# Queries and keys as block products, and attention's steps regrouped among the k tiles

## The chip, the cores and the metric

The kernel runs on one core of a Trainium2 chip. The metric is the time of one execution on the device, in microseconds (us). The median of three runs of the kernel before is 1344.37 us (1343.51 to 1346.86).

## What is computed

One layer of a decoder for two groups of tokens, 512 of a new prompt and 8 x 8 of samples with a paged past, 576 together, at a model width of 1024, all in float32:

```python
h = _rmsnorm(x, g_attn)
zq, zk, zv, zu, zs, zm, zg = jnp.split(h @ w_in, offs, axis=-1)
o_da = _da_prompt(q, k, v, ...)        # 8 heads; p1 - lam * p2, both softmax; RMSNorm of each head's output
o_sg, vn = _spatial_gate(jax.nn.gelu(zu), jax.nn.gelu(zs), sg_norm, sg_w, sg_b)
o_mx = _cross_attn(zm, mem_k, mem_v)   # 4 heads into 256 memory tokens
merged = gates[0] * (o_da @ w_branch[:1024]) + gates[1] * (o_sg @ ...) + gates[2] * (o_mx @ ...)
x = x + merged @ w_out
a, b = jnp.split(_rmsnorm(x, g_ffn) @ w_up, 2, axis=-1)
x = x + (jax.nn.silu(a) * b) @ w_down
```

`zq` and `zk`, `h` times two 1024 x 1024 blocks of `w_in`, are computed first and are used by the differential attention of prompt and samples; `zk` and `zv` are outputs too.

## The kernel before

**Panels.** Every product with a weight is cut into panels: 128 output features by 576 tokens, kept transposed (features on the partitions). `T` is 576, `HT` half of it, 288; `KT` is 8, the number of 128-row k tiles of the width. Float32 precision comes from a split: weights and activations are each a rounded high part and a low remainder, and each product is hi*hi + hi*lo + lo*hi. A k tile of a panel is therefore 3 x 2 matmuls of 128x288, and a panel of 8 k tiles is 48 matmuls (`panel`, L1895). Two accumulator pairs `acc[0]`, `acc[1]` alternate by panel. `split_hi` (L696, ACT) rounds the weights of the panel two ahead into `w_hi`, `split_lo` (L1183, DVE) subtracts that from `w_raw` into `w_lo`; SP (`stream`, `load_w`) loads `w_raw`, one DMA per panel of 0.5 MB, after the `w_lo` before it in that buffer is made. ACT evacuates a finished panel.

**Stages.** `STAGES` lists them: `mk`, `mv` (keys and values of the memory), `s` (spatial gate's v half, 8 panels), `q`, `k`, `v`, `u`, `da_gate` (8 panels each), `sg_branch` (16), `zm`, `da_proj`, `mx_gate`, `mx_proj`, `w_out` (8 each), then the feed-forward net: `up` and `down`. Behind the panels stand the smaller matmuls: `turn_tile` transposes a tile of `s` and `v` into token order (DVE's `nat_copy` takes it out), `mix` (L2053) does the spatial gate's 128x128 products behind the `k` panels, each waiting for its predecessor's `mix_bias` on DVE.

**Pairs.** The `up` stage has another form. A unit computes a pair of panels of 22 (`FT`) with a seven-product scheme for 2x2 blocks: the four blocks are two halves of the width by two 288-token halves, combined into sums and differences on both sides. A unit is `NJ` = 7 products of 4 (`KH`) k tiles and three matmuls each, 84 instead of 96 (`product`, L2349). For it DVE forms the weight sums (`pair_sums`) and low parts (`lo_of`), ACT the high parts (`hi_of`, L1061) and copies of products 0, 1 and 2 (`product_copy`, L1070), and DVE adds the products from PSUM into the two outputs. The activations' sums are made once (`xs_raw`, `xs_hi`, `xs_lo`). The weight sums of the first unit are formed on POOL (L1873) after the last `w_out` panel but one. All engines' loops over units are written out by hand and meet by counters: `pair_hi_done`, `pair_lo_done`, `pair_mm`, `pair_copied`, `pair_out`. At the end of the last unit ACT and DVE split the weights of down panels 0 and 1; then `g_hi` (ACT, L1137) and `g_lo` (DVE, L1684) tiles are made, and the first down panel (`down_panel`, L2376) waits for each k tile of them.

**Attention behind the gate panels.** Prompt attention is 32 tiles (`TILES_P`), four query blocks for each of eight heads, in the order `TILE_ORDER` of widths; tile n is in head n // 4. For a tile: `p_score` (L2088, TensorE, two products into two banks), `p_logits` (DVE, L1369, a minimum of each row), `p_exps` (ACT, L843), `p_combine` (DVE, L1394 to L1402, gives `a_p`), `p_turn_probs` (TensorE, L2098, transposes `a_p`, one to four blocks), `p_turned` (ACT, L866, copy to `aT_p`), `p_values` (TensorE, L2107). For a head: `p_copy` (ACT, L872), `p_squares` (ACT, L880), `p_norm` (DVE, L1409), `p_turn_out` (TensorE, L2079) and `p_output` (ACT, L886). There is one score buffer: `p_score(n)` waits for `p_logits(n-1)`. There is one turn buffer: `p_turn_probs(n)` waits for the `aT_p` copy of n-1. TensorE puts a step in front of each k tile of the gate panels: `p_step(q)` with q = 8c + k - 2 for k tile k of panel c. ACT and DVE have the same steps in program order, with each panel's evacuation (L702), `split_hi` and `split_lo` among them, so a step that comes late on one of them holds what stands behind it. The samples' attention follows behind `sg_branch`, the memory attention behind `da_proj` (samples) and `mx_gate` (prompt: `prompt_step(h, slot)`, 16 slots for a head in two panels, with `c_score` L2272, `c_turn_p` L2282, `c_values` L2288). `m_turn_o` (L2247) turns a sample's `o_m`, which DVE makes (L1501).

## Time and profile before

| | |
|---|---|
| median of three runs | 1344.37 us |
| the profiled execution | 1343.05 us |
| its span | 1341.3 us |
| TensorE busy | 98% of the span |
| VectorE (DVE) busy | 50% |
| ScalarE (ACT) busy | 39% |
| GpSimd (POOL) busy | 7% |
| DMA, mean over the span | 134 GB/s |
| granted TensorE clock, mean | 0.992 |

The span is the time between the first and the last record; what lies around it (1.75 us) is start and end. In a timeline each row is one instruction, or several of one kind that follow each other, with the time of its start, its length, engine, line, operation and tiles; in square brackets stands the idle time of the engine before it and the engine that ended it. Lengths of matmuls in sequence overlap, so distances are read from start to start. PE is TensorE.

### The profile page before, as it was taken

How to read it: one execution, taken by the hardware profiler on the slowest of the kernel's cores; microseconds unless marked ns; L12 is line 12 of the kernel's file. 1: busy time of each engine (PE TensorE's matmuls, PEld its weight loads, DVE VectorE, ACT ScalarE, POOL GpSimd, SP SyncE). 2: the span in 40 equal slices, each digit the busy share in tenths (PEclk: the TensorE clock that was granted, in tenths of full speed). 3: DMA queues.
4: the chain of work that ended last, by engine and by line, in shares of the span. 5: the costliest groups of instructions: out<-in, count | busy, mean ns of one | idle time of the engine just before them, and what ended most of it. 6: DMA issues, size and time to landing. Idle time of an engine off the chain costs nothing.

```text
span 1341.3 us, 25811 instructions
## 1 busy us (share of the span) xinstructions
PE 1315.5 (98%) x10082; PEld 1245.4 (93%) x10082; DVE 667.9 (50%) x1167; ACT 524.5 (39%) x1010; POOL 89.9 (7%) x129
## 2 busy tenths in 40 slices
PE   8899999999999999999999999998999999999997
PEld 8889999999888888888988889998999999999997
DVE  6643232223566532222344323567888888863333
ACT  5432321223477632222422343245555555552220
POOL 3620000000001010000000000001000000000001
PEclk9999999999999999999999999998999999999998
DMA  6544222524222197776589111432222222222221
GB/s 240 165 154 163 81 87 76 197 102 150 71 75 71 53 304 226 260 247 207 195 321 342 61 48 48 148 106 72 93 94 94 94 94 94 94 79 90 84 94 71
DMA packets 82087, 179.10 MB, mean 134 GB/s; under 512 B 5869, under 2 KB 40941, under 8 KB 80982
## 3 DMA queue, kind: packets, MB, share of 16 engines
q1 hardware_dynamic: 77750, 158.31, 34.7%
q10 hardware_dynamic: 2496, 12.58, 2.6%
q0 software_dynamic: 1760, 7.08, 1.5%
q8 instruction: 57, 0.93, 0.3%
q14 instruction: 24, 0.20, 0.0%
HBM read 166.13 MB, written 14.18 MB: 134 GB/s over the span
## 4 chain that ended last, share of the span: by engine, by line
PE 62%; issue 31%; DVE 2%; POOL 2%; ACT 1%; DMA 1%; POOLq 0%; SPq 0%; DVEq 0%; ACTq 0%
PE acc L1895 49%; PE ps L2107 2%; PE ps L2088 2%; PE ps L2164 1%; PE ps L2141 1%; PE ps L2272 1%; POOL ssum L1765 1%; PE ps L2288 1%; PE ps L2098 1%; PE ps L2239 1%; PE ps L1922 1%; PE ps L2053 1%; PE ps L2221 1%; DVE w_lo L1183 0%; DMA m_x<-memT 0%
## 5 line engine op out<-in xcount | busy, mean ns | idle before, releaser
L1183 DVE TENSOR_TENSOR w_lo<-w_raw,w_hi 128x1024 fp32r<-128x1024 f32 x144 | 178.0, 1236 | 369.7 <-ACT w_hi L696 368.8
L1895 PE MATMUL acc<-h_hi,w_hi 128*128 128x288 f32 x1152 | 263.2, 310 | 2.5 <-POOL h_lo L1745 2.4
L1895 PE MATMUL acc<-h_lo,w_hi 128*128 128x288 f32 x1152 | 247.5, 296 | 0.0
L1895 PE MATMUL acc<-h_hi,w_lo 128*128 128x288 f32 x1152 | 247.3, 296 | 0.0
L696 ACT ACTIVATE w_hi<-w_raw 128x1024 fp32r<-128x1024 f32 x144 | 152.0, 1056 | 156.4 <-PE acc L2376 74.6
L1895 PEld LDWEIGHTS acc<-h_hi,w_hi 128*128 128x128 f32 x1152 | 183.2, 189 | 13.8 <-issue 9.1
L1895 PEld LDWEIGHTS acc<-h_hi,w_lo 128*128 128x128 f32 x1152 | 184.7, 188 | 0.0
L1895 PEld LDWEIGHTS acc<-h_lo,w_hi 128*128 128x128 f32 x1152 | 184.7, 188 | 0.0
L2349 PE MATMUL acc<-xs_hi,w_hi 128*128 128x288 f32 x352 | 105.2, 299 | 3.5 <-DVE x_sb L1595 3.5
L2349 PE MATMUL acc<-xs_lo,w_hi 128*128 128x288 f32 x352 | 105.5, 300 | 0.0
L2349 PE MATMUL acc<-xs_hi,w_lo 128*128 128x288 f32 x352 | 105.4, 299 | 0.0
L2349 PE MATMUL acc<-xs_hi,w_hi_b 128*128 128x288 f32 x264 | 77.5, 294 | 0.9 <-issue 0.9
L2349 PE MATMUL acc<-xs_hi,w_lo_b 128*128 128x288 f32 x264 | 78.0, 296 | 0.0
L2349 PE MATMUL acc<-xs_lo,w_hi_b 128*128 128x288 f32 x264 | 77.8, 295 | 0.0
L2376 PE MATMUL acc<-g_lo,w_hi 128*128 128x288 f32 x352 | 75.7, 296 | 0.0
L2349 PEld LDWEIGHTS acc<-xs_hi,w_hi 128*128 128x128 f32 x352 | 67.3, 191 | 3.8 <-issue 3.8
L1895 PE MATMUL acc<-m_hi,w_hi 128*128 128x256 f32 (+1 forms) x256 | 65.4, 296 | 4.9 <-DVE w_lo L1183 4.3
L2349 PEld LDWEIGHTS acc<-xs_lo,w_hi 128*128 128x128 f32 x352 | 67.4, 191 | 0.0
L2349 PEld LDWEIGHTS acc<-xs_hi,w_lo 128*128 128x128 f32 x352 | 67.2, 191 | 0.0
L2376 PE MATMUL acc<-g_hi_main,w_hi 128*128 128x288 f32 x304 | 65.4, 296 | 0.0
L2376 PE MATMUL acc<-g_hi_main,w_lo 128*128 128x288 f32 x304 | 65.4, 296 | 0.0
L1895 PE MATMUL acc<-m_lo,w_hi 128*128 128x256 f32 (+1 forms) x256 | 64.0, 291 | 0.0
(330 smaller groups left out, 2410.6 us busy)
## 6 DMA issues: line engine op xcount, KB each, us to landing
w_raw<-w_stream SPq DMA_DIRECT2D x166, 512.0 KB, 3.5
v_pg<-cache_v SPq DMA_DIRECT2D x32, 512.0 KB, 5.5
w_raw_b<-w_stream SPq DMA_DIRECT2D x22, 512.0 KB, 4.2
k_even<-cache_k SPq DMA_DIRECT2D x16, 512.0 KB, 6.6
k_odd<-cache_k SPq DMA_DIRECT2D x16, 512.0 KB, 6.7
km_pg<-mem_k ACTq DMA_DIRECT2D x6, 1024.0 KB, 7.2
vm_pg<-mem_v ACTq DMA_DIRECT2D x6, 1024.0 KB, 7.3
x_sb<-xT SPq DMA_DIRECT2D x8, 576.0 KB, 6.0
```

The source lines that it names most:

```text
L696: nc.scalar.activation(w_hi[:, u, :], w_raw[:, u, :], ACT.Copy).then_inc(w_hi_done, 1)
L1183: nc.vector.tensor_tensor(w_lo[:, u, :], w_raw[:, u, :], w_hi[:, u, :].bitcast(F32), ALU.subtract)\
L1765: nc.gpsimd.tensor_tensor(ssum[:, :], sq_slot[0] if k == 1 else ssum[:, :], sq_slot[k % 2], ALU.add)\
L1895: last = nc.tensor.matmul(acc[a][:, c, 0:n], w[:, u, k * P:(k + 1) * P], x[:, k0 + k, c * n:(c + 1) * n], start=start and k == 0 and t == ...
L1922: last = nc.tensor.transpose(bank(4 + u)[:, j * P:(j + 1) * P], turn[:, u, j * P:(j + 1) * P], ident)
L2053: nc.tensor.matmul(bank(4 + u)[:, j * P:(j + 1) * P], s_nat[:, j, n * P:(n + 1) * P], sg_w[:, n, :], start=True, stop=True)
L2088: last = nc.tensor.matmul(bank(4 + c)[:, 0:w], qT[rows, h, i * P:(i + 1) * P], kT[rows, h, 0:w], start=True, stop=True)
L2098: last = nc.tensor.transpose(bank(6)[:, j * P:(j + 1) * P], a_p[:, m, j * P:(j + 1) * P], ident)
L2107: last = nc.tensor.matmul(bank(7)[:, i * DV:(i + 1) * DV], aT_p[:, m, j * P:(j + 1) * P], v_nat[:, j, h * DV:(h + 1) * DV], start=j == 0, ...
L2141: last = nc.tensor.matmul(bank(4 + c)[rows, 0:HK], q_blk[:, h, :], k_slot[e][:, h, c * HK:(c + 1) * HK], start=lane == 0, stop=lane == 1)
L2349: last = nc.tensor.matmul(pair_bank(j, s), w[:, k * P:(k + 1) * P], x[:, k, X_KIND[j], :], start=BANK_START[j] and k == 0 and t == 0, stop ...
L2376: last = nc.tensor.matmul(acc[a][:, c, 0:HT], w[:, u, k * P:(k + 1) * P], x[:, c * HT:(c + 1) * HT], start=start and k == 0 and t == 0, st ...
```

## The change

- `q` and `k` leave `STAGES` and become eight units `qk` in `PAIRS`, between `s` and `v`: units 0 to 3 give `qT`, 4 to 7 `kT`, two panels each. The products' banks are exchanged at unit 4 (`SWAP`). The activations' sums and differences of `h` are made by POOL during the `s` panels and split by ACT (`ht_split`) and DVE (`ht_low`); the first unit's weight sums by POOL (`first_sums`). The outputs are written by DVE with the scale in the instruction. The weights of `w_in` for `q` and `k` are streamed in pairs. The mixes stand behind the `v` panels; the normalisation of `s` stands in units 3 to 7 (DVE) and its squares in units 1 and 2 (ACT). The loads of the spatial gate's constants and the first `key_pages` wait for other counters.
- `p_step`: `p_score`, `p_values` and `p_turn_probs` all stand in even slots, values two slots later and turns one slot later relative to the scores; `p_turn_out` one slot later. The loops of ACT and DVE for these steps are not edited.
- The first `up` unit: its weights are loaded between the `w_out` loads, its sums and splits are made two panels earlier; TensorE waits for the two accumulators apart.
- `prompt_step`: slot 0 has only `m_values`, slot 1 `m_turn_o` and both `c_score`, slot 12 both `c_values`.
- The last `up` unit: down panel 0 is split behind product 4, down panel 1 behind product 6 and after the silu and the last output; SP's stream of `down` begins once all low parts of the units are made.

```diff
-STAGES = (("mk", 8), ("mv", 8), ("s", 8), ("q", 8), ("k", 8), ("v", 8), ("u", 8), ("da_gate", 8),
+STAGES = (("mk", 8), ("mv", 8), ("s", 8), ("v", 8), ("u", 8), ("da_gate", 8),
           ("sg_branch", 16), ("zm", 8), ("da_proj", 8), ("mx_gate", 8), ("mx_proj", 8), ("w_out", 8), ("down", 24))
 FIRST = {}
...
-PAIRS = (("up", FT),)
+PAIRS = (("qk", KT), ("up", FT))
...
 BANK_OF = ("x", "z", "x", "z", "x", "w", "x")
+T_OF = {1: 0, 4: 1, 5: 2, 6: 3}
+SWAP = QK // 2
+XD, XH = 6 * KH, KH
...
-            stream(FIRST["s"] + 6, FIRST["q"] + 2)
-
-            sp.wait_ge(mm_done, FIRST["s"] + 1)
+            stream(FIRST["s"] + 6, FIRST["v"], 0)
+            sp.wait_ge(w_lo_done, FIRST["v"])
+            load_pair(1, 0, STREAM_AT["qk"])
+
...
+            load_pair(2, 1, STREAM_AT["qk"])
...
+            for i in range(3, QK):
+                load_pair(i, 1 - i % 2, STREAM_AT["qk"])
+            sp.wait_ge(pair_lo_done, NJ * QK)
+            stream(FIRST["v"], FIRST["v"] + 4)
...
-            sp.wait_ge(g_bias, KT)
+            sp.wait_ge(pair_mm, NJ * QK)
...
-            stream(FIRST["w_out"] + 2, FIRST["down"])
+            stream(FIRST["w_out"] + 2, FIRST["w_out"] + 6)
+            sp.wait_ge(o_lo_done, 4 * KT)
+            load_pair(QK, 1, STREAM_AT["up"])
...
-            sp.wait_ge(pair_lo_done, NJ * (FT - 1))
+                    load_pair(2 * i + e, 1 - e, STREAM_AT["up"])
...
+                if 2 <= n < 2 + KH:
+                    ht_split(n - 2)
+                for j in ((0, 1, 2), (3, 4), (5, 6))[n - 5] if n >= 5 else ():
+                    hi_of(j, 0, 1)
...
+            for i in range(QK):
+                s, t, last = 1 - i % 2, i % 2, i == QK - 1
+                for c in range(3):
+                    product_copy(c, i, s, -(DK ** -0.5) if i < SWAP else 1.0)
+                    if not last:
+                        hi_of(c, i + 1, t)
+                if last:
+                    for u in range(2):
+                        act.wait_ge(pair_mm, NJ * i + 2 * u + 5)
+                        split_hi(FIRST["v"] + u, u)
+                else:
+                    hi_of(3, i + 1, t)
+                    if i == 1:
+                        act.wait_ge(nat_done, 2 * KT)
+                        nat_square_tile(0)
+                        nat_square_tile(1)
+                    if i == 2:
+                        nat_square_tile(2)
+                        nat_square_tile(3)
+                        nat_square_tile(4).then_inc(g_ss, 1)
+                    for j in (4, 5, 6):
+                        hi_of(j, i + 1, t)
...
+                if n == KT - 3:
+                    for j in (0, 1, 2):
+                        hi_of(j, QK, 1)
...
-                    for u in range(2):
-                        act.wait_ge(pair_mm, NJ * (FT - 1) + 2 * u + 2)
-                        split_hi(FIRST["down"] + u, u)
+                    act.wait_ge(pair_mm, NJ * i + 5)
+                    split_hi(FIRST["down"], 0)
...
+                else:
+                    act.wait_ge(pair_mm, NJ * i + 7)
+                    split_hi(FIRST["down"] + 1, 1)
...
+            def ht_low(k):
+                dve.wait_ge(x_hi, k + 1)
+                nc.vector.tensor_tensor(ht_lo[:, k], ht_raw[:, k], ht_hi[:, k].bitcast(F32), ALU.subtract).then_inc(x_lo, 1)
...
+            for i in range(QK):
+                s, t, last = 1 - i % 2, i % 2, i == QK - 1
+                dst, a = (qT, 2 * i) if i < SWAP else (kT, 2 * (i - SWAP))
+                scale = -(DK ** -0.5) if i < SWAP else 1.0
+                if not last:
+                    lo_of(0, i + 1, t)
+                    pair_sums(1, i + 1, t)
+                    pair_sums(2, i + 1, t)
+                    lo_of(1, i + 1, t)
...
+                dve.wait_ge(pair_mm, NJ * i + 4)
+                dve.wait_ge(pair_copied, 3 * i + 3)
+                nc.vector.scalar_tensor_tensor(dst[:, a, HT:T], pair_bank(3, i, s), scale, square[:, 0:HT],
+                                               ALU.mult, ALU.add).then_inc(pair_out, 1)
+                if not last:
+                    pair_sums(3, i + 1, t)
+                    lo_of(2, i + 1, t)
...
+                if 3 <= i < 3 + QT:
+                    nat_norm(i - 3)
+                if i == 3 + QT:
+                    nat_norm(QT).then_inc(g_norm, 1)
...
-                    split_lo(FIRST["down"] + 1, 1)
+                    split_lo(FIRST["down"], 0)
...
-                if not last:
+                nc.vector.tensor_tensor(g_tile[:, 0:HT], gate[:, 0:HT], pair_bank(6, i, s), ALU.mult).then_inc(pair_out, 1)
+                if last:
+                    split_lo(FIRST["down"] + 1, 1)
...
+            for k in range(KH):
+                x1, x2 = gate[:, :], square[:, :]
+                t1, t2, t3, t4 = (ht_raw[:, k, m, :] for m in range(4))
+                wait(pool, x_diff, 6 * k)
+                nc.gpsimd.tensor_tensor(x1, h_hi[:, k, :].bitcast(F32), h_lo[:, k, :].bitcast(F32), ALU.add).then_inc(x_diff, 1)
+                nc.gpsimd.tensor_tensor(x2, h_hi[:, KH + k, :].bitcast(F32), h_lo[:, KH + k, :].bitcast(F32), ALU.add)\
+                    .then_inc(x_diff, 1)
+                pool.wait_ge(x_diff, 6 * k + 2)
+                nc.gpsimd.tensor_tensor(t1, x1[:, HT:T], x1[:, 0:HT], ALU.subtract).then_inc(x_diff, 1)
+                nc.gpsimd.tensor_tensor(t3, x2[:, HT:T], x1[:, HT:T], ALU.subtract).then_inc(x_diff, 1)
+                pool.wait_ge(x_diff, 6 * k + 4)
+                nc.gpsimd.tensor_tensor(t2, t3, x1[:, 0:HT], ALU.add).then_inc(x_diff, 1)
+                pool.wait_ge(x_diff, 6 * k + 5)
+                nc.gpsimd.tensor_tensor(t4, x2[:, 0:HT], t2, ALU.subtract).then_inc(x_diff, 1)
...
+            first_sums(0, FIRST["v"])
...
+            for i in range(QK):
+                for j in range(NJ):
+                    if i == 0 and j == 1:
+                        pe.wait_ge(acc_free[1], FIRST["v"] // 2)
+                    product(j, i, 1 - i % 2)
+                    if i == 0 and j == 2:
+                        turn_tile("s", KT - 1, 1, KT)
...
+                u = n % 2
+                if n < 2:
+                    pe.wait_ge(pair_out, 4 * QK - 1 + n)
+                slot_free("v", n // 2, u)
+                panel(FIRST["v"] + n, u, h_hi, h_lo)
+                if n:
+                    pe.wait_ge(g_bias, n)
+                    turn_tile("v", n - 1, 1 - u, 2 * KT)
+                wait(pe, nat_done, 2 * KT + n - 1)
...
-                wait(pe, p_oout, len([h for h in range(HEADS) if 8 * h + 16 < 2 * n + 3]))
+                wait(pe, p_oout, len([h for h in range(HEADS) if 8 * h + 17 < 2 * n + 4]))
...
             def p_step(q):
 
-                n = (q - 3) // 2
-                if q % 2 == 0 and 0 < q // 2 < TILES_P - 1:
-                    p_score(q // 2 + 1)
-                if q % 2 and 0 <= n < TILES_P:
-                    p_turn_probs(n)
-                if q % 2 == 0 and 4 <= q <= 2 * TILES_P + 2:
-                    p_values(q // 2 - 2)
-                if q % 8 == 0 and 0 <= q // 8 - 2 < HEADS:
+                n = q // 2
+                if q % 2 == 0:
+                    if 0 < n < TILES_P - 1:
+                        p_score(n + 1)
+                    if 0 <= n - 3 < TILES_P:
+                        p_values(n - 3)
+                    if 0 <= n - 2 < TILES_P:
+                        p_turn_probs(n - 2)
+                elif q % 8 == 1 and 0 <= q // 8 - 2 < HEADS:
                     p_turn_out(q // 8 - 2)
...
             def prompt_step(h, slot):
-                if slot == 0:
+                if slot == 0 and h == 0:
+                    m_values(NB - 1)
+                elif slot == 1:
                     if h == 0:
-                        m_values(NB - 1)
                         pe.wait_ge(kv_loaded, 32)
                         pe.wait_ge(m_exp, NB)
+                        pe.wait_ge(m_o, NB)
+                        m_turn_o(NB - 1)
                     c_score(h, 0)
-                elif slot == 2:
-                    if h == 0:
-                        pe.wait_ge(m_o, NB)
                     c_score(h, 1)
-                    if h == 0:
-                        m_turn_o(NB - 1)
                 elif slot == 9:
                     if h == 0:
                         pe.wait_ge(m_oout, NB)
                     c_turn_p(h)
-                elif slot in (12, 13):
-                    c_values(h, slot - 12)
+                elif slot == 12:
+                    c_values(h, 0)
...
-            all_evacuated(pe, "down")
             for j in range(NJ):
-                product(j, 0, 0, first=True)
+                if j < 2:
+                    pe.wait_ge(acc_free[j], FIRST["down"] // 2)
```

## Rows read from the trace of the kernel before

**Rows 1.** The page's first part: busy time, share of span, instructions

```profile
PE 1315.5 (98%) x10082; PEld 1245.4 (93%) x10082; DVE 667.9 (50%) x1167; ACT 524.5 (39%) x1010; POOL 89.9 (7%) x129
```

**Rows 2.** Chain of waits, whole span: start us, length us, what

```profile
88.86 6.40 PE acc L1895 x48
```

**Rows 3.** Chain of waits: two POOL operations on a k tile of h

```profile
77.80 2.78 POOL h_lo L1745 x2
```

**Rows 4.** Busy times in a stretch of `up`: PE, PEld, DVE, ACT, POOL, clock, DMA

```profile
990.00:1100.00 110.00, 110.00 (x830) 110.00 (x830) 93.29 (x168) 59.46 (x109) 0.00 (x0) 1.00 0.26 95
```

**Rows 5.** Timeline of TensorE, one head in `da_gate`: start us, length us, line, operation

```profile
403.18 1.13 PE L2088 MATMUL ps<-kT,qT 64*128 64x512 f32 x4
...
412.04 0.42 PE L1895 MATMUL acc<-h_hi,w_lo 128*128 128x288 f32 x2
412.55 0.63 PE L2098 MATMUL ps<-cst,a_p 128*128 128x128 f32 x4
...
413.91 0.70 PE L2088 MATMUL ps<-kT,qT 64*128 64x256 f32 x4
...
416.34 0.27 PE L2098 MATMUL ps<-cst,a_p 128*128 128x128 f32 x1
...
417.34 1.13 PE L2088 MATMUL ps<-kT,qT 64*128 64x512 f32 x4
418.40 0.49 PE L2107 MATMUL ps<-v_nat,aT_p 128*128 128x128 f32 x2
418.64 0.52 PE L1895 MATMUL acc<-h_hi,w_hi 128*128 128x288 f32 x2
...
419.53 0.49 PE L2098 MATMUL ps<-cst,a_p 128*128 128x128 f32 x3
...
420.75 0.49 PE L2088 MATMUL ps<-kT,qT 64*128 64x128 f32 x4
421.17 0.94 PE L2107 MATMUL ps<-v_nat,aT_p 128*128 128x128 f32 x6
```

**Rows 6.** Timeline of ACT, the same stretch

```profile
413.21 0.60 ACT L866 ACTIVATE aT_p<-ps 128x512 f32<-128x512 f32 x1
...
414.24 1.06 ACT L696 ACTIVATE w_hi<-w_raw 128x1024 fp32r<-128x1024 f32 x1
...
416.83 0.59 ACT L872 ACTIVATE scaled<-ps 128x512 f32<-128x512 f32 x1
```

**Rows 7.** Timeline of DVE, the same stretch

```profile
415.33 1.22 DVE L1183 TENSOR_TENSOR w_lo<-w_raw,w_hi 128x1024 fp32r<-128x1024 f32 x1 [1.27 <-ACT w_hi L696]
...
416.81 0.42 DVE L1369 CUSTOM_DVE_ANT_0 logit_p<-ps,square 128x256 f32<-128x256 f32 x1
...
421.84 0.28 DVE L1369 CUSTOM_DVE_ANT_0 logit_p<-ps,rms_b 128x128 f32<-128x128 f32 x1
```

**Rows 8.** Timelines of TensorE and DVE, start of `mx_gate`

```profile
741.78 1.99 PE L2272 MATMUL ps<-kmT,zmT 128*128 128x256 f32 x8
...
744.22 0.48 DVE L1501 TENSOR_SCALAR o_m<-ps,small 128x256 f32<-128x256 f32 x1
```

**Rows 9.** Timelines of DVE, ACT and TensorE, end of the last `up` unit

```profile
1179.93 0.45 DVE L1666 TENSOR_TENSOR scaled<-cp,acc 128x288 f32<-128x288 f32 x1
...
1182.66 6.77 DVE L1684 TENSOR_TENSOR g_lo<-g_sb,g_hi_main 128x576 fp32r<-128x576 f32 x10
...
1181.20 0.69 ACT L1129 ACTIVATE gate<-scaled 128x576 f32<-128x576 f32 x1 [3.40 <-DVE scaled L1670]
...
1183.71 0.43 PE L2376 MATMUL acc<-g_hi_main,w_hi 128*128 128x288 f32 x2
```

**Rows 10.** Timeline of TensorE at `up`'s start; busy times in two stretches

```profile
929.60 0.58 PE L2349 MATMUL acc<-xs_hi,w_hi 128*128 128x288 f32 x1 [3.55 <-DVE x_sb L1595]
...
929.60:935.40 5.80, 5.80 (x24) 5.80 (x25) 4.97 (x10) 5.18 (x10) 0.00 (x0) 0.50 0.00 0
...
78.00:82.00 4.00, 2.44 (x16) 2.20 (x17) 0.00 (x0) 0.50 (x2) 3.04 (x3) 1.00 0.03 11
```

447 lines of the change are left out of this document (237 added, 210 removed).

## The prediction

> **What bounds the kernel now.** I first read the page's busy shares: TensorE is busy for 1315.5 of 1341.3 us over 10082 matmuls, 98% [rows 1]. So the end is set by TensorE's own instructions, and an edit is worth what it removes there plus what waiting it adds. The chain of waits, followed back from the end, is mostly TensorE's own work too, and gives the price of a panel: 48 matmuls take 6.40 us, 0.133 us each [rows 2]. Where no other engine is shown as releaser, slack on DVE, ACT and the DMA queues is worth nothing; but their fixed order decides how late a result comes, so the timeline of one attention head in the `da_gate` panels was read engine by engine [rows 5 to 7]. The profiled execution took 1343.05 us (span 1341.3 and 1.75 around it); the median is 1.3 us above it. The sum below is against 1343.05, and 1.3 is added at the end. A measurement of this kernel can tell about 0.3% from no change, so "same" means 1340.3 to 1348.4 us.
>
> **A. Queries and keys as products.** Sixteen panels of 48 matmuls (768) become eight units of 7 x 12 (672): 96 fewer. In the `up` stage, which already works so, a stretch of 110.00 us holds 830 matmuls, 0.1325 each [rows 4]; a panel's are 0.1333 [rows 2]. 96 x 0.1333 = **-12.8 us**. The mixes only move from the `k` panels to the `v` panels, with the same evacuations, and a panel of 6.40 us hides them as before: nothing. The Trainium skill (TensorE: Matmul & The Clock Gate, section Back-to-back issue gap) gives sustained spacings of about 81 ns at 128 columns and 131 ns at 512; a straight line between them makes an estimate of 102 ns at 288 columns, by which part A would bring 9.8 us, not 12.8. The trace has 133 ns at 288 columns, and the measurement decides.
>
> What feeds the units is hidden if DVE and ACT keep up. In `up` they do, with DVE busy for 93.29 and ACT for 59.46 of 110.00 us [rows 4] and TensorE never idle. A qk unit has fewer combining operations than an `up` unit (no gate product, no silu), so nearly the same load; five normalisations of 128x1024 come on top, one in each of units 3 to 7. The nearest row of that width is the 1.22 us `split_lo` [rows 7]: a unit of 11.2 us at 85% leaves 1.7 us free, so they just fit. POOL's half sums run during the `s` panels, four groups of six operations; two of its operations on a k tile of `h` take 2.78 us [rows 3], so 24 take 33 us at most, and eight panels last 51. A DMA of a pair is the 1 MB of two panels, as in `up`. Entry, exit and these: 0 to +8 us (five normalisations and the evacuations at the two ends all exposed), I take **+0.3**, nearest to the `up` row.
>
> **B. Attention's steps behind fewer k tiles.** This is the part that costs. `p_step` works off three chains. Before, score(n+1) and values share the even k tiles and turn_probs the odd ones; now all three stand in the even ones, and turn_probs comes one k tile later relative to the scores, values two. ACT's and DVE's loops of this stretch are untouched, in their order.
>
> First chain. At 412.55 TensorE turns the 512-wide probabilities (4h+7). ACT's queue takes, in order, the copy `aT_p` (413.21), the gate's evacuation, `split_hi` (414.24); DVE's `split_lo` waits for that (415.33) and the two logits of tile 4h+10 stand behind it, the second at 416.81 for 0.42 [rows 5 to 7]. Only when these are read is the score bank free: score(4h+11) starts at 417.34, a hand-over of 0.11 later. From turn to score that is 4.79 us, and before it was just covered by two k tiles and the other steps. After the change only the four-matmul turn with its k tile (412.55 to 413.91, 1.36) and one plain k tile (6 x 0.133 = 0.80) lie between turn and score: 2.16. 4.79 - 2.16 = 2.63 us of wait per head. The last head has no next scores: 7 x 2.63 = **+18.4**.
>
> Second chain. The turn of 4h+8 (one block, 416.34) is followed on ACT by the `aT_p` copy, the copy of the head's output (416.83), its four squares and the two exponentials of 256, on DVE by the combination, the head's normalisation and the logits of 4h+12, the second at 421.84 for 0.28 [rows 5 to 7]: 422.12, with the hand-over 422.23, 5.89 us after the turn. TensorE has between the two after the change: turn and tile 416.34 to 417.34 = 1.00, a tile 0.80, the 128-wide score 0.42 (420.75 to 421.17), values 0.24 (418.40 to 418.64), a three-block turn and tile 1.22 (419.53 to 420.75), a tile 0.80: 4.48 [rows 5]. Wait 1.41 us, in six heads **+8.5**.
>
> What gathering gives back: the output's turn moves from slot 8h+16 to 8h+17, so its copy to `qT` is out of the way of the next probabilities; TensorE stands there now: the pair of matmuls at 412.04 is through at 412.31 (2 x 0.133), the turn starts at 412.55 [rows 5]. 7 x 0.24 = **-1.7**. Standing alone costs a turn nothing that I can find: a one-block turn and its k tile take 1.00 (416.34 to 417.34), a k tile after a switch 0.89 (418.64 to 419.53). Bounds 0 to -2.9 (8 heads x 4 x 0.09), I take 0. Part B: **+25.2 us**; a head's period, 14.16 now (403.18 to 417.34, [rows 5]), becomes about 17.8.
>
> **C. The first `up` unit.** Its weights are loaded and split earlier, between the loads of `w_out`. SP waits for `o_lo_done` ahead of `w_out`'s last two panels, which is long reached. But what TensorE waits for at 929.60 is `x_sb`, the last evacuation of `w_out` (idle 3.55) [rows 10], and that stays. The next 24 matmuls run at granted clock 0.50. At most one split is taken off the tail. **-0.5**, bounds -2 (half of the idle time) and +1 (late load).
>
> **E. `prompt_step`.** The last sample's output is now turned in slot 1, ahead of the prompt's scores. It needs `o_m` from DVE, which runs at 744.22 for 0.48 behind a split and the two merge operations [rows 8]; with a hand-over of 0.11 it is there at 744.81. TensorE comes to it after m_values and one tile, 741.78 + 0.89 (a k tile after a switch) = 742.67. Before, two score groups and two tiles lay in front. **+2.1**.
>
> **F. The last `up` unit.** ACT's and DVE's splits of down panels 0 and 1 are put later: panel 0 behind the fifth product (which ends at 1181.32 - 3.20 = 1178.12), panel 1 behind the last. 1178.12 + 1.06 + 1.22 [rows 6, 7] + 0.2 of hand-overs = 1180.60, when DVE can begin what begins at 1179.93 now [rows 9]. That puts ACT's silu from 1181.20 to 1181.86; 0.6 later ACT splits panel 1 (1.06) until 1183.5, DVE (1.22) until 1184.7, and only then comes the first `g_lo` of the main buffer. One takes 0.7 (6.77 / 10): ready at 1185.4. TensorE asks for it at 1183.71 [rows 9]; now it is ready at 1182.66 + 0.7. **+1.7**; bounds 0 and +2.5.
>
> **Sum.** -12.8 + 0.3 + 25.2 - 0.5 + 2.1 + 1.7 = +16.0: 1359.05 for the profiled execution, 1360.4 us for the median. Slower, 1.2%.
>
> **The rivals.**
> *The waits don't arise* (the other side: faster). If the `da_gate` chains are shorter than what TensorE has between turn and score, part B is -1.7 or less. For it: the copy at 413.21 has no idle time before it, so ACT arrives there about when the turn is done, and a chain that starts from ACT's own queue would not slip with the turn. It decides at 2.16 us for the first and 4.48 for the second. Against: the rows have 4.79 and 5.89, every member is fixed in program order, and none is edited. Time: 1360.4 - 25.2 = 1335.2, down to 1331 without E and F. Chance 0.07.
> *Half the waits.* The first chain loses the part of ACT's queue that starts early and the second vanishes: +12 instead of +25.2, 1347. Chance 0.05, of which 0.04 within 0.3% and 0.01 faster.
> *The clock falls after the new waits.* After an idle time of 3.55 us the granted clock is 0.50 (1.2 of 2.4 GHz) and 24 matmuls take 5.80 us [rows 10], 0.24 each, 2.6 us over full speed. A wait of 2.63 us with transposes around it in each of seven heads would add 7 x 2.6 = 18: 1378. Against: in the stretch 78 to 82 TensorE is busy for 2.44 of 4.00 us, and the clock stays 1.00 [rows 10]. Chance 0.07. The Trainium skill (same page, section Part 4: PE-mode transpose) says transposes don't count as busy in the same way as matmuls do, which speaks for this rival; no row here shows transposes alone beside a low clock.
> *The qk units saturate DVE*, by the bound of part A: 5 to 6 us more, 1366. For it: 85% busy before the normalisations [rows 4]. Chance 0.05.
> My own forecast has 0.76.
>
> **How the numbers follow.** Around 1360.4: B1 holds to within 0.5 us per head (3.5), E and F may be nothing (-3.8), the entry to the qk units and C swing by 2; together about -8 and +7.6, which takes in the saturated rival. Range 1352 to 1368; outside are the first rival, half waits and the clock, 0.19 together. Slower by over 0.3%: 0.76 + 0.07 + 0.05 = 0.88. Same: 0.04. Faster: 0.07 + 0.01 = 0.08.
>
> **What would show it.** A: 672 matmuls at the new product line in front of `v`, 11.2 us a unit, with no idle time. B: in the `da_gate` panels DVE's logits as releaser of the 512-wide score with about 2.6 us idle, and of the score two tiles after it with about 1.4; a period near 17.8 us; TensorE at full granted clock. E: one idle of 2.1 us in front of the transposes of `o_m`. F: one idle of 1.7 us in front of the third or fourth k tile of the first down panel. The prediction is wrong if the period stays near 14: then ACT's order was not what held the score, and the kernel ends below 1336.

## The result, and the profile after

The changed kernel takes 1370.58 us (median of 4 runs, 1368.75 to 1372.14) against 1344.29 us for the kernel before, now over four: 1.0191 of the time before, 95% interval 1.0177 to 1.0205. The forecast was 1360.4, range 1352 to 1368: the direction was right, the size too small, and the time lies 2.6 us above the range. The profiled execution took 1369.95 us, its span is 1368.0. One execution of the kernel with the old `prompt_step` below ran at a mean granted clock of 0.556 and took 2100.12 us; it is left out of that kernel's median.

Busy shares on the page of the changed kernel:

```profile
PE 1315.1 (96%) x9986; PEld 1242.9 (91%) x9986; DVE 726.4 (53%) x1271; ACT 546.9 (40%) x1062; POOL 126.6 (9%) x157
```

There are 96 matmuls fewer than in [rows 1], and TensorE's busy time is nevertheless the same, 1315.1 against 1315.5 us: some of its work ran slower. Its share has fallen from 98 to 96%. What TensorE waited for (the line that waited, the engine and line it waited for, us in total, times, longest):

```profile
PE ps L2248 <- DVE small L1497: 23.8, 14, 2.5
...
PE acc L2187 <- DVE x_sb L1696: 2.5, 1, 2.5
...
PE ps L2063 <- DVE ssum L1277: 1.6, 1, 1.6
PE acc L2514 <- DVE g_lo L1778: 1.5, 1, 1.5
PE ps L2408 <- DVE o_m L1629: 1.5, 1, 1.5
...
PE acc L2187 <- DVE xs_lo L1704: 0.7, 1, 0.7
```

The first row is the large one: 14 waits, 23.8 us, in front of `p_score` (L2248), for DVE's logits (L1497); the kernel before had none on that pair. The others are the first `up` unit (2.5, 1.6, 0.7), the first down panel (1.5) and the turn of `o_m` (1.5).

Since both traces have the same landmarks on TensorE, the 26.7 us by which the spans differ can be split by stretch. Each number is the time from one landmark to the next, after less before:

| stretch on TensorE | forecast | measured |
|---|---|---|
| start to the first `s` panel | 0 | +2.0 |
| `s`, queries and keys, `v`, `u` up to the first score | -12.5 | -13.2 |
| `da_gate` (first score to the samples' first score) | +25.2 | +32.2 |
| `sg_branch`, `zm`, `da_proj` | 0 | 0.0 |
| `mx_gate` to the end of `w_out` | +2.1 | +2.4 |
| first `up` unit, up to its third product | -0.5 | +0.6 |
| rest of `up` | 0 | +1.0 |
| the first three k tiles of `down` | +1.7 | +1.7 |
| rest | 0 | 0.0 |

The attention stretch was read in the sixth head, as in [rows 5] for the fourth. TensorE in the changed kernel:

```profile
436.64 0.43 PE L2012 MATMUL acc<-h_hi,w_lo 128*128 128x288 f32 x2
439.60 2.08 PE L2248 MATMUL ps<-kT,qT 64*128 64x512 f32 x4 [2.53 <-DVE small L1497]
441.61 2.07 PE L2267 MATMUL ps<-v_nat,aT_p 128*128 128x128 f32 x8
443.48 0.42 PE L2258 MATMUL ps<-cst,a_p 128*128 128x128 f32 x1
443.55 0.83 PE L2012 MATMUL acc<-h_hi,w_hi 128*128 128x288 f32 x2
```

The 512-wide score starts at 439.60 after 2.53 us of idle time; it was released by DVE. And then something shows that the forecast left out: the score takes 2.01 us from start to start (439.60 to 441.61) where the same four matmuls took 1.06 before (417.34 to 418.40 in [rows 5]), and the first two matmuls of the k tile behind it take 0.83 instead of about 0.5. TensorE runs at half its clock for a while. In three of the seven waiting heads the score itself is slow like this, in three more what stands behind it (see the last section), and in the first of them (365.18) nothing is. What it waited for, on ACT and on DVE:

```profile
435.52 0.60 ACT L942 ACTIVATE aT_p<-ps 128x512 f32<-128x512 f32 x1 [1.06 <-PE ps L2258]
...
436.54 1.06 ACT L733 ACTIVATE w_hi<-w_raw 128x1024 fp32r<-128x1024 f32 x1
```

```profile
437.63 1.22 DVE L1242 TENSOR_TENSOR w_lo<-w_raw,w_hi 128x1024 fp32r<-128x1024 f32 x1 [2.29 <-ACT w_hi L733]
...
439.12 0.42 DVE L1497 CUSTOM_DVE_ANT_0 logit_p<-ps,rms_b 128x256 f32<-128x256 f32 x1
```

This is the first chain of the prediction member by member, now from 434.9, the turn's place ahead of ACT's copy at 435.52: `split_hi` at 436.54, `split_lo` at 437.63, the logits' second half from 439.12 to 439.54, the score at 439.60. Its members have the lengths of [rows 6, 7]; only TensorE arrives earlier.

The clock over six heads, each row with the stretch, its length, the busy times of PE, PEld, DVE, ACT and POOL with counts, the granted clock and the DMA share:

```profile
365.18:478.72 113.54, 93.51 (x588) 75.92 (x588) 54.79 (x187) 61.99 (x192) 8.45 (x18) 0.91 0.16 56
```

Six heads take 113.54 us, 18.9 each, at a mean granted clock of 0.91 (the levels are 1.2 and 2.4 GHz, 0.50 and 1.00). In the kernel before they take 14.16 each.

### The profile page after: what moved, and what is told of

Its sections match the earlier page's. It is cut to its first block, busy times and chain, and to the rows that moved or that the text cites. A ratio compares the mean times of both kernels' runs of the same rounds, so it can differ in the third digit from the quotient of the medians.

```text
span 1368.0 us, 25775 instructions
## 1 busy us (share of the span) xinstructions
PE 1315.1 (96%) x9986; PEld 1242.9 (91%) x9986; DVE 726.4 (53%) x1271; ACT 546.9 (40%) x1062; POOL 126.6 (9%) x157
## 4 chain that ended last, share of the span: by engine, by line
PE 58%; issue 32%; DVE 4%; ACT 3%; POOL 2%; DMA 1%; POOLq 0%; SPq 0%; ACTq 0%; DVEq 0%
PE acc L2012 38%; PE acc L2187 7%; PE ps L2267 2%; PE ps L2248 2%; PE ps L2325 1%; PE ps L2302 1%; PE ps L2433 1%; POOL ssum L1859 1%; PE ps L2449 1%; ACT w_hi L733 1%; DVE logit_p L1497 1%; ACT p_junk L956 1%; PE ps L2258 1%; PE ps L2039 1%; PE ps L2209 1%
## 5 line engine op out<-in xcount | busy, mean ns | idle before, releaser
L1242 DVE TENSOR_TENSOR w_lo<-w_raw,w_hi 128x1024 fp32r<-128x1024 f32 x128 | 161.0, 1258 | 307.8 <-ACT w_hi L733 307.3
L2012 PE MATMUL acc<-h_hi,w_hi 128*128 128x288 f32 x896 | 205.2, 311 | 2.5 <-POOL h_lo L1839 2.4
L733 ACT ACTIVATE w_hi<-w_raw 128x1024 fp32r<-128x1024 f32 x128 | 135.2, 1056 | 167.6 <-PE acc L2514 74.9
L2012 PE MATMUL acc<-h_lo,w_hi 128*128 128x288 f32 x896 | 193.7, 298 | 0.0
L2012 PE MATMUL acc<-h_hi,w_lo 128*128 128x288 f32 x896 | 193.4, 297 | 0.0
L2012 PEld LDWEIGHTS acc<-h_hi,w_hi 128*128 128x128 f32 x896 | 144.0, 191 | 12.2 <-issue 7.6
L2012 PEld LDWEIGHTS acc<-h_lo,w_hi 128*128 128x128 f32 x896 | 145.1, 190 | 0.0
L2012 PEld LDWEIGHTS acc<-h_hi,w_lo 128*128 128x128 f32 x896 | 144.7, 190 | 0.0
L844 ACT ACTIVATE w_hi<-w_sum 128x512 fp32r<-128x512 f32 x60 | 37.8, 632 | 67.0 <-DVE w_sum L1389 40.3
```

The lines of the kernel that those rows point to most:

```text
L733: nc.scalar.activation(w_hi[:, u, :], w_raw[:, u, :], ACT.Copy).then_inc(w_hi_done, 1)
L844: nc.scalar.activation(pair_hi(j, i), pair_part(j, i, s), ACT.Copy).then_inc(pair_hi_done, 1)
L1242: nc.vector.tensor_tensor(w_lo[:, u, :], w_raw[:, u, :], w_hi[:, u, :].bitcast(F32), ALU.subtract)\
L2012: last = nc.tensor.matmul(acc[a][:, c, 0:n], w[:, u, k * P:(k + 1) * P], x[:, k0 + k, c * n:(c + 1) * n], start=start and k == 0 and t == ...
```

## The experiments

The first two questions are where the 32 us come from, and which part of them is waiting and which is the clock.

**The old steps in the changed kernel.** `p_step` and the matching count in `p_turn_probs` as before:

```diff
-                n = q // 2
-                if q % 2 == 0:
-                    if 0 < n < TILES_P - 1:
-                        p_score(n + 1)
-                    if 0 <= n - 3 < TILES_P:
-                        p_values(n - 3)
...
+                n = (q - 3) // 2
+                if q % 2 == 0 and 0 < q // 2 < TILES_P - 1:
+                    p_score(q // 2 + 1)
+                if q % 2 and 0 <= n < TILES_P:
+                    p_turn_probs(n)
...
```

> The changed kernel with `p_step` (and the matching count in the turn's wait) as it was before: everything else of the change stays. Theory (the regrouped steps cost TensorE two waits per head and, behind them, a fallen clock): the `da_gate` stretch gives back 32 us, time 1370.6 - 32 = 1338 us, a head's period 14.2 us, no idle time in front of the scores, mean granted clock back at about 0.99. Rival (the qk units leave ACT, DVE or the DMA queues behind, and the gate panels inherit it): part of the waits stays, time above 1350.

Measured: 1340.53 us (1337.44 to 1340.85), 0.9958 of the kernel before [0.9944, 0.9972]. The stretch `da_gate` is back at its old length (0.0 us against before), the heads at 14.16, and in one window over the last seven heads the clock is whole:

```profile
365.25:464.00 98.75, 98.19 (x704) 80.82 (x707) 60.78 (x201) 72.79 (x225) 10.80 (x23) 1.00 0.21 74
```

All of the +32.2 us hang on `p_step`. The qk units leave nothing behind. Between the medians the new steps cost 30.1 us (1370.58 less 1340.53).

**The new steps in the kernel before.** The same edit the other way round, queries and keys as 16 panels.

> The kernel before with only the new `p_step`: queries and keys still as 16 panels. Theory: the same waits as in the changed kernel, 2.5 us in front of the 512-wide score of each head and 0.3 to 1.2 us in front of the 384-wide one, and the clock falls behind them: 1344.3 + 32 = 1376 us. Rival (the waits need the qk units): 1344 to 1355 us.

Measured: 1377.57 us (1371.67 to 1381.35), 1.0228 [1.0198, 1.0257]; 14 waits of 24.0 us in front of the scores, `da_gate` +34.0 us. The waits don't need the qk units either.

**The wait filled.** What TensorE does while it would stand still:

```diff
                 w = (i + 1) * P
+                if n % QT == 3 and n > QT:
+                    pe.wait_ge(p_aT, n - 3)
+                    for _ in range(18):
+                        nc.tensor.matmul(bank(6)[:, 0:HT], w_hi[:, h % 2, 0:P], h_hi[:, 0, 0:HT], start=True, stop=True)
                 wait(pe, p_logit, n)
```

> The changed kernel; in front of the 512-wide score of heads 1 to 7, 18 extra matmuls of 128x288 (2.4 us at full clock) are issued into the free turn bank, where TensorE otherwise stands for 2.5 us. They compute nothing that is used. It separates waiting from the clock. Theory (about 9 us of the 32 are the clock that falls behind the waits): the waits are covered but not shortened, the clock in the stretch stays at 1.00, the period falls from about 19 to about 17.8, the time to 1370.6 - 9 = 1361 us. Rival (the clock falls for transposes and small matmuls, not for the wait, or costs nothing): the time stays at 1370 or rises.

Measured: 1363.42 us (1363.21 to 1364.94), 1.0141 [1.0124, 1.0158]: 7.2 us less than the changed kernel, with more work. TensorE in the fourth and fifth head (start, length, line, operation), and then six heads in one window:

```profile
397.93 0.43 PE L2012 MATMUL acc<-h_hi,w_lo 128*128 128x288 f32 x2
398.20 2.56 PE L2248 MATMUL ps<-h_hi,w_hi 128*128 128x288 f32 x18
400.88 1.13 PE L2252 MATMUL ps<-kT,qT 64*128 64x512 f32 x4
...
408.79 0.92 PE L2252 MATMUL ps<-kT,qT 64*128 64x384 f32 x4 [1.20 <-DVE small L1497]
...
418.65 0.70 PE L2252 MATMUL ps<-kT,qT 64*128 64x512 f32 x2
```

```profile
365.34:471.95 106.61, 98.62 (x697) 83.28 (x697) 54.64 (x187) 61.76 (x192) 8.44 (x18) 1.00 0.17 60
```

The filling (x18) ends where the score may start, the 512-wide score takes its 1.13 again, the clock stays at 1.00, and the period is 17.77 us (400.88 to 418.65). The forecast for this quantity was 17.8. So the waits were sized about rightly, and the 7 to 8 us beyond them are the clock: `da_gate` is +24.1 us here and +32.2 in the changed kernel. The 384-wide score now shows its full wait, 1.20 us in each of six heads, 7.2 in all; in the changed kernel it had 0.3 to 1.2, 4.9 in all, since the slowed TensorE arrived later.

The Trainium skill (TensorE: Matmul & The Clock Gate, section Part 4: PE-mode transpose) says that transposes don't count as busy in the way matmuls do. Here the same transposes stand at the same places in both kernels and the clock falls only in the one that also waits; by this pair it is the wait that decides. Whether a transpose counts as busy the pair can't tell.

**The split behind the logits.** One member of the first chain is taken out of DVE's order:

```diff
                 if 0 < n < TILES_P - 1:
                     p_logits(n + 1)
+                if n % QT == 1 and n > QT:
+                    split_lo(FIRST["da_gate"] + n // QT + 1, (n // QT - 1) % 2)
                 p_combine(n)
...
-                if n % QT == 0 and n:
-                    split_lo(FIRST["da_gate"] + n // QT + 1, (n // QT - 1) % 2)
```

> The changed kernel; on DVE the gate stage's `split_lo` stands behind the logits of tile 4h+10 instead of ahead of them, nothing else. It cuts the first chain at one member: the logits no longer wait for ACT's evacuation and `split_hi`. Theory: the 2.5 us wait in front of the 512-wide score is gone in every head, its clock loss too, and the second chain's wait of the 384-wide score comes out at its full 1.2 to 1.4 us: period about 15.5, time 1370.6 - 17.7 - 9 + 3 = 1347 us. Rival (the score waits for something else, or the wait moves to the next step with the same size): 1362 us or more.

Measured: 1345.26 us (1343.46 to 1346.78), 1.0000 [0.9990, 1.0009]. That is 25.3 us less than the changed kernel, of the 30.1 us that the new steps cost: one edit of order on another engine. What TensorE waited for in front of the scores, and the scores of one head:

```profile
PE ps L2248 <- DVE small L1497: 8.2, 13, 1.3
```

```profile
392.90 1.13 PE L2248 MATMUL ps<-kT,qT 64*128 64x512 f32 x4
...
397.36 0.49 PE L2248 MATMUL ps<-kT,qT 64*128 64x128 f32 x4 [0.54 <-DVE small L1497]
...
400.81 0.92 PE L2248 MATMUL ps<-kT,qT 64*128 64x384 f32 x4 [0.62 <-DVE small L1497]
...
408.10 1.13 PE L2248 MATMUL ps<-kT,qT 64*128 64x512 f32 x4
```

The 512-wide score has no idle time before it, the second chain's wait is spread over two scores (0.54 and 0.62), and the period is 15.2 us (392.90 to 408.10). The 4.7 us that are still missing against the old steps are these waits, less what gathering gives back (`da_gate` is 6.0 us longer in the trace than with the old steps). With waits no longer than 1.3 us the clock of the stretch stays at 1.00.

**The turns back, the values left.** Which of the two moves does it? The turn of a head's output goes back to its old slot with the others.

```diff
                     if 0 <= n - 3 < TILES_P:
                         p_values(n - 3)
-                    if 0 <= n - 2 < TILES_P:
-                        p_turn_probs(n - 2)
-                elif q % 8 == 1 and 0 <= q // 8 - 2 < HEADS:
-                    p_turn_out(q // 8 - 2)
+                    if q % 8 == 0 and 0 <= q // 8 - 2 < HEADS:
+                        p_turn_out(q // 8 - 2)
+                elif 0 <= (q - 3) // 2 < TILES_P:
+                    p_turn_probs((q - 3) // 2)
```

> The changed kernel with the turns back in the odd k tiles (2n+3, as before), the values left two slots later as in the change. It tells which of the two moves lengthens the wait. Theory (the score waits because the turn comes later relative to it): between the 512-wide turn and the next 512-wide score TensorE has 1.36 + 1.76 + 1.00 = 4.12 us of work again against a chain of 4.79: a wait of 0.7 us instead of 2.5, no fallen clock, period about 14.9; 1340.5 + 7 x 0.7 = 1345 us. Rival (the later values hold the copies and the bank, so that the waits stay): above 1360 us.

Measured: 1348.94 us (1347.08 to 1350.79), 1.0032 [1.0022, 1.0042]. A 512-wide score and the turn two tiles on:

```profile
393.92 1.13 PE L2248 MATMUL ps<-kT,qT 64*128 64x512 f32 x4 [0.34 <-DVE small L1497]
...
400.52 0.44 PE L2258 MATMUL ps<-cst,a_p 128*128 128x128 f32 x2 [0.83 <-DVE a_p L1530]
```

The wait of the 512-wide score has gone from 2.53 to 0.34: it was the later turn that made it. The expectation missed by 4 us, because the later values have a price of their own: they hold ACT's copy of the head's output, the exponentials behind it and DVE's combination, for which the turn at 400.52 waits 0.83 us (8 such waits, 7.5 us in all; 1, of 1.2, with the old steps). Period 15.6.

**The first `up` unit, the down split, the prompt's steps.** These were taken one by one, on top of the kernel with the old steps. The start of `up` in the changed kernel, on DVE and then on TensorE:

```profile
951.24 0.75 DVE L1277 TENSOR_TENSOR ssum<-ssum,square 128x576 f32<-128x576 f32 x1
951.90 0.68 DVE L1397 TENSOR_TENSOR w_lo_b<-w_sum_b,w_hi_b 128x512 fp32r<-128x512 f32 x1
952.50 1.28 DVE L1397 TENSOR_TENSOR w_lo<-w_sum,w_hi 128x512 fp32r<-128x512 f32 x2
953.71 0.75 DVE L1696 TENSOR_TENSOR x_sb<-acc,x_sb 128x576 f32<-128x576 f32 x1
...
958.55 0.75 DVE L1277 TENSOR_TENSOR ssum<-ssum,gate 128x576 f32<-128x576 f32 x1
...
954.51 0.61 PE L2187 MATMUL acc<-xs_hi,w_hi_b 128*128 128x288 f32 x1 [2.48 <-DVE x_sb L1696]
...
959.35 1.28 PE L2063 MATMUL ps<-cst,ssum 128*128 128x1 f32 x10 [1.59 <-DVE ssum L1277]
960.49 0.38 PE L2187 MATMUL acc<-xs_hi,w_hi_b 128*128 128x288 f32 x1
```

and DVE's last evacuation in the kernel before:

```profile
928.75 0.74 DVE L1595 TENSOR_TENSOR x_sb<-acc,x_sb 128x576 f32<-128x576 f32 x1
```

There it started 2.9 us after TensorE's last `w_out` matmuls (which ended at 925.89); now it starts 4.4 us after them (949.28), because three low parts of the `up` weights (951.90 and the pair at 952.50, 1.8 us together) stand ahead of it. The kernel before had two there as well (1.2 us). The edit:

```diff
                 add_square(n, u, 2)
-                if n >= KT - 3:
-                    if n < KT - 1:
-                        first_lows(QK, n - (KT - 3))
+                if n == KT - 3:
+                    first_lows(QK, 0)
+            first_lows(QK, 1)
             first_lows(QK, 2)
```

> The changed kernel with the old `p_step`, and on DVE the low parts 2 to 4 of the first `up` unit behind the last `w_out` evacuation and its square sum instead of ahead of them. Theory (these three, 1.8 us, hold the last evacuation and with it the last activations, the square sum and the norm): the last `x_sb` comes 1.8 us earlier relative to the end of `w_out`, and the time falls by 1.6 to 1.8 from the 1340.5 us of the old steps: 1338.8. Rival (the low parts are then late for product 2, the gain is given back): 1340.5.

Measured: 1336.18 us (1335.81 to 1337.38), 0.9939 [0.9924, 0.9953], 4.3 us less than with the old steps alone. In the trace the stretch from `w_out`'s end to the third product has shrunk by 2.6 us, from 12.0 to 9.4; the rest is no more than the two medians' spread. TensorE stands 3.0 us in front of the norm's matmuls, as with the old steps alone: the square sum is what comes last.

For the down panels, ACT's and DVE's split of panel 1 go behind the eighth tile:

```diff
             for k in range(G_LATE, FT):
+                if k == 8:
+                    split_hi(FIRST["down"] + 1, 1)
...
             for k in range(G_LATE, FT):
+                if k == 8:
+                    split_lo(FIRST["down"] + 1, 1)
```

> As the kernel with the low parts later, and the split of down panel 1 on ACT and DVE behind the eighth tile of the gated activations instead of ahead of the fourth. Theory: the 1.5 us wait at the fourth k tile of the first down panel is gone and none comes at the second panel: 1337.2 us. Rival (panel 1's weights are then late): the wait moves to the second down panel, 1338.8 or more.

Measured: 1335.28 us (1333.35 to 1336.47), 0.9925 [0.9910, 0.9941]. The 1.5 us wait is 0.2 and none comes at the second panel: the stretch is 1.35 us shorter. The medians differ by 0.9 and the profiled spans not at all (1334.2 against 1334.0), so the time alone would not show it.

And `prompt_step` gets its old slots back:

```diff
-                if slot == 0 and h == 0:
-                    m_values(NB - 1)
-                elif slot == 1:
+                if slot == 0:
                     if h == 0:
+                        m_values(NB - 1)
                         pe.wait_ge(kv_loaded, 32)
                         pe.wait_ge(m_exp, NB)
-                        pe.wait_ge(m_o, NB)
-                        m_turn_o(NB - 1)
                     c_score(h, 0)
+                elif slot == 2:
+                    if h == 0:
+                        pe.wait_ge(m_o, NB)
                     c_score(h, 1)
+                    if h == 0:
+                        m_turn_o(NB - 1)
...
```

> As the one before, with `prompt_step` as it was before the change: only the product form of queries and keys and the earlier start of `up` stay of the change. Theory: the wait of about 1.8 us for `o_m` is gone, with 2.3 us in all: 1334.9 us. Against the kernel before that is the 13.2 us of the products plus some 0 to 3 us of start-up that differs between executions. Rival (the wait was covered by a later one): 1337.

Measured: 1332.83 us (median of five, 1331.93 to 1334.38), 0.9914 [0.9901, 0.9928]. The two forecasts below call this kernel the one of 1333.4 us, the median with the sixth execution in it. The wait for `o_m` is gone and its stretch is back at its old length (2.4 us less). This kernel beats both: 11.5 us under the kernel before (1344.38 in the same comparison), 38 under the changed one. The gain is the product form's. From `w_out`'s end to `down` this kernel takes 256.8 us against 255.4 in the kernel before, and the other four with the mended order take 255.8 to 256.5: the earlier start of `up` brings nothing, even mended.

**The square sum first.** For the last `w_out` panel the square and its sum go directly behind the evacuation:

```diff
+                if n == KT - 1:
+                    resid_square(n, u, 2, tile)
                 nc.scalar.activation(scaled[:, u, :], x_sb[:, tile, :], ACT.Copy,
...
+                if n == KT - 1:
+                    add_square(n, u, 2)
                 dve.wait_ge(x_gained, n + 1)
```

> The kernel of 1333.4 us, and for the last of `w_out`'s panels the square and its addition to the sum directly behind the evacuation instead of behind the splits of the activations. Theory (since the early start of `up`, TensorE waits 3.0 us for the square sum): that wait goes and about 0.5 to 1 us comes at product 2 for activations split later; time 1331.5. Rival (the norm's chain behind it or the splits hold TensorE as long): 1333.4.

Measured: 1333.04 us (1331.13 to 1333.50), 0.9913 [0.9897, 0.9930]: no change against 1332.83. TensorE's norm matmuls and the third product:

```profile
919.73 1.17 PE L2068 MATMUL ps<-cst,ssum 128*128 128x1 f32 x10
923.37 0.40 PE L2192 MATMUL acc<-xs_hi,w_hi_b 128*128 128x288 f32 x1 [2.47 <-DVE w_lo_b L1399]
```

The wait for the square sum is gone, as forecast, but 2.47 us of wait for the low part of product 2's weights stand behind it, since those are made after the activations' splits. The rival was right: in both orders that were tried DVE's work between the last evacuation and product 2 holds TensorE.

**Gathering without its waits.** The kernel of 1333.4 us with the new `p_step` and a mended order on both engines:

```diff
                     p_exps(n + 1)
+                if n % QT == 1 and n > QT:
+                    p_squares(n // QT - 1)
                 p_turned(n)
...
-                    p_squares(n // QT - 1)
...
-                p_combine(n)
-                if n % QT == 2 and n > QT:
+                if n % QT == 3 and n > QT:
                     p_norm(n // QT - 1)
+                p_combine(n)
```

(and `split_lo` behind the logits, as above).

> The kernel of 1333.4 us (old `prompt_step`, later lows and later down split), but with the new, gathered `p_step`, and ACT's and DVE's order mended for it: `split_lo` behind the logits of tile 4h+10, the four squares behind the exponentials of tile 4h+10, the head's normalisation behind the logits of 4h+12. It tells whether gathering is worth anything once its waits are gone. Theory (gathering itself gives TensorE next to nothing; only fixed order on ACT and DVE made the waits): no wait over 0.5 us in front of a score, period 13.9 to 14.2 us against 14.16, time 1332 to 1334. Rival (fewer switches are worth 0.1 us for each of 32 tiles or more): period 13.7 or less, 1330 or less. Rival (new waits elsewhere): above 1337.

Measured: 1335.15 us (1334.65 to 1335.46), 0.9931 [0.9914, 0.9947]. The scores of one head with a wait, and the next:

```profile
406.30 1.13 PE L2248 MATMUL ps<-kT,qT 64*128 64x512 f32 x4
...
410.75 0.49 PE L2248 MATMUL ps<-kT,qT 64*128 64x128 f32 x4 [0.54 <-DVE small L1497]
...
420.81 1.13 PE L2248 MATMUL ps<-kT,qT 64*128 64x512 f32 x4
```

The period is 14.51 us (406.30 to 420.81) with one wait of 0.54, so 13.97 without it, against 14.16 for the old steps: gathering the steps gives TensorE 0.2 us per head at best, less than the one wait it still causes. It is worth nothing here: the kernel is 2.3 us slower than with the old steps, and so is the stretch `da_gate` in the trace. The expectation of no wait over 0.5 us and 1332 to 1334 us was missed: there are seven waits, 1.28 us in the first head and 0.52 to 0.88 in the others.

## Why the prediction was wrong in size

**Queries and keys (right).** Forecast -12.5, measured -13.2. A window in the qk units of the changed kernel:

```profile
140.00:220.00 80.00, 80.00 (x605) 80.00 (x604) 62.38 (x106) 42.16 (x78) 2.07 (x3) 1.00 0.22 80
```

605 matmuls (two of them only reach into the window) in 80 us without idle time, 0.133 each, at full clock, with DVE at 78% and ACT at 53%: the feeding is hidden, as in [rows 4], and the rival of a saturated DVE is out. Of the 0.7 us more than forecast, 0.4 are the spacing: 96 matmuls less at 0.1333 was the forecast, but the 672 of the units stand a little closer too, 89.2 us in all, 0.1328 each. The other 0.3 is the term for entry and exit, which did not show. The units take the same time in all ten profiles that have them; the whole stretch is 11.7 to 13.2 us shorter than before, because in some of these executions the clock falls in the `s` panels ahead of them (see below).

**The two chains (right).** Waits of 2.63 and 1.41 us were forecast, 2.53 and 1.20 measured (1.20 in the kernel with the filled wait, where the clock is whole). With a 1.28 us wait in the first head, which the forecast lacked, the waits add up to 26.2 us, gathering gives back 2.1, and the sum is +24.1 us against +25.2. The agreement of the period, 17.77 with 17.8, is partly luck: 17.8 is the 25.2 us spread over seven heads, and for a head with both waits the forecast's own terms give 14.16 + 2.63 + 1.41 - 0.24 = 17.96. The rival that they don't arise is refuted, and so is the rival that half arises; the run with `split_lo` moved shows the first chain's cause, the run with the turns moved shows that the later turn triggers it.

**The clock (the step that failed).** The prediction had "the clock falls after the new waits" as a rival with chance 0.07, priced at 18 us, and held against it a stretch in which TensorE was busy for 2.44 of 4.00 us at a clock of 1.00 [rows 10]. It fell. Behind the waits of the later heads the score or the tile after it ran at half clock, and the cost is 32.2 - 24.1 = 8.1 us, 7.2 between the medians. The waits alone would have left the forecast standing: the kernel with the filled wait takes 1363.42 us, inside the range. Both readings of the rows were off. The first is the row held against the clock's fall. Its longest wait is 1.75 us, not 2.5, and one execution of it proved little. Here is that stretch in the kernel before, and then in the profile of the kernel with the square sum first, where the last row is a window with its granted clock, 0.50, as in [rows 10]:

```profile
79.26 0.54 PE L1895 MATMUL acc<-h_hi,w_hi 128*128 128x288 f32 x2 [1.75 <-POOL h_lo L1745]
...
80.63 0.53 PE L1895 MATMUL acc<-h_hi,w_hi 128*128 128x288 f32 x2 [0.31 <-POOL h_lo L1745]
```

```profile
79.71 0.53 PE L2017 MATMUL acc<-h_hi,w_hi 128*128 128x288 f32 x2 [1.75 <-POOL h_lo L1844]
...
81.09 0.85 PE L2017 MATMUL acc<-h_hi,w_hi 128*128 128x288 f32 x2 [0.32 <-POOL h_lo L1844]
...
81.00:84.00 3.00, 2.91 (x12) 2.90 (x13) 0.00 (x0) 0.62 (x2) 0.49 (x2) 0.50 0.00 0
```

The same wait at the same place, and there the clock fell to 0.50. It fell at this place in seven of the twelve profiles, and stayed at 1.00 in five, the kernel before among them. The one row of the kernel before with a wait longer than 2.5 us, 3.55 us before `up`, did show 0.50 [rows 10]. The second is the price, 24 slow matmuls or 2.6 us at each of seven waits. The cost was 1.2 us at each, net: with 7.2 - 4.9 = 2.3 us added that the slower TensorE took back at the second chain's waits, 1.5. A forecast of the waits plus half the rival's price would have been 1369. Not every wait costs the clock: behind 2.51 us at the first 512-wide score after the first head (365.18) it stayed at 1.00 and the score took 1.13. That is not a property of the place. In the kernel before with the new steps the same wait of 2.51 us (379.53) did cost it: the score took 1.79 us. So the fall differs between executions; in the two profiles 13 of 14 such waits cost the clock. What decides it in one execution stays open.

**The first `up` unit (wrong sign).** Forecast -0.5, measured +0.6, and +1.0 behind it. I had taken the last evacuation as fixed ("and that stays"). It was not: the earlier low parts were put ahead of it in DVE's order. The bounds, -2 to +1, took in its first half only. The second half is mostly the clock again, 0.83 in the ten us behind the norm's wait. The profiled execution was a good one here: over the five profiles with this code the two together are +1.6 to +3.2 us.

**`prompt_step` and the last unit (right).** +2.1 forecast and +2.4 measured; +1.7 and +1.7. The turn of `o_m` in the changed kernel, and the first down panel with what DVE does ahead of it:

```profile
762.45 1.07 PE L2400 MATMUL ps<-vm_pg,pT_mb 128*32 128x256 f32 x16 [0.57 <-issue]
...
765.99 0.41 PE L2408 MATMUL ps<-cst,o_m 128*128 128x128 f32 x2 [1.48 <-DVE o_m L1629]
```

```profile
1208.47 1.23 DVE L1242 TENSOR_TENSOR w_lo<-w_raw,w_hi 128x1024 fp32r<-128x1024 f32 x1
1209.62 4.09 DVE L1778 TENSOR_TENSOR g_lo<-g_sb,g_hi_main 128x576 fp32r<-128x576 f32 x6
...
1210.42 0.54 PE L2514 MATMUL acc<-g_hi_main,w_hi 128*128 128x288 f32 x2 [1.54 <-DVE g_lo L1778]
```

The wait at 765.99 is 1.48 us. The 0.57 us in front of `m_values` (L2400), for which the trace names no releaser, are a part of the same 2.1: TensorE comes that much later to `o_m`. In all seven profiles with the new `prompt_step` the two add up to 1.9 to 2.1 us. The fourth k tile starts 1.54 us late, at 1210.42, as `split_lo` stands ahead of `g_lo` at 1208.47. Both were undone without a new wait in their place.

**The start.** 2.0 us of the profiled difference lie ahead of the first `s` panel. In the profiles of the nine other kernels that share this start it is 0.5 to 2.3 us, and 1.6 in a tenth, the kernel before with the new steps, whose code there is unchanged. It differs between executions and is not the change's.

Summed up, of the 10.7 us between the forecast and the profiled difference, 8.1 are the clock in `da_gate`, 2.1 the start of `up` and 2.0 the start; the products and the chains' sizes took back 1.8, and `prompt_step` added 0.3.

## What to carry to other kernels

When a step moves on one engine, follow the program order of the engines that answer it: a split or a square that was harmless ahead of a result becomes the release of the next step, and moving that one instruction (here `split_lo` behind the logits) can bring back most of the loss, 25.3 of 30.1 us. Grouping small steps to save switches is worth only what a switch costs in the trace, 0.2 us a head here, and that is to be weighed against each result coming later. And a wait of TensorE has two prices, its length and the matmuls behind it at half clock: where the trace shows a low clock behind a wait of that size, take it into the sum and not among the unlikely rivals. A row in which the clock kept up in one execution is weak evidence against it: read the same place in several profiles first.

## What the runs showed of the hardware

Filling a wait with unused matmuls made the kernel faster: 126 matmuls more and 7.2 us less, with the granted clock at 1.00 instead of 0.91 over six heads. With waits of up to 1.3 us and otherwise the same transposes the clock stayed at 1.00. The fall came about at the wait's end in some heads (the score took 2.08 us at 401.43) and one to one and a half us behind it in others (the score at 420.82 took its 1.13, and the window 420.80 to 427.00 has a clock of 0.72), so the score behind a wait doesn't tell by itself whether the wait costs the clock. The same wait need not cost the same in the next execution: behind a wait of 1.75 us in the `s` panels the clock fell to 0.50 in seven of twelve profiles, and behind waits of 1.5 to 2.1 us for `o_m` in one of six (2.11 us, with the split behind the logits).
